# Four norms of a two-block transformer kernel: the eighth tile's squares summed on TensorE, the function table loaded ahead, and the second norm in three operations a tile

## The chip, the cores and the metric

The kernel is one program on one core of a Trainium2 chip. The time is the device time of that core in microseconds, the median of several executions. The engines are PE (TensorE), DVE (VectorE), ACT (ScalarE), POOL (GpSimd) and SP (SyncE), which run their own instruction streams and meet only at semaphores.

## The reference

Two transformer blocks run one after the other on a batch of one, with 512 tokens of 1024 channels in fp32. What matters here are four root-mean-square norms over the 1024 channels, each of which stands between two matrix products:

```python
x = x + gate1 * (merged @ w_o)                         # first block
y = rms_norm(x, norm2_w) * (1 + scale2) + shift2       # second norm
x = x + gate2 * ((gelu(conv(y @ up_a)) * (y @ up_v)) @ ffn_w_down)
xn = rms_norm_2(h, norm1_g)                            # third norm, second block
proj = xn @ w_in
...
h = h + merged @ w_out
hn = rms_norm_2(h, norm2_g)                            # fourth norm
ff = square(relu(hn @ w_ff1)); h = h + ff @ w_ff2
hg = rms_norm_2(h, norm3_g)                            # fifth norm
h = h + sigmoid(hg @ w_ple_gate + b) * (p @ w_ple)
```

with `rms_norm(x, w) = x * rsqrt(mean(x * x) + 1e-6) * w`.

## The kernel before

The activations lie transposed: a tile is 128 channels by 512 tokens, and eight tiles make the 1024 channels (`XR[0..7]` holds the residual stream). Every product is done in three passes: a weight block `wraw` is split into a rounded part `whi` (by ACT) and its remainder `wlo` (by DVE or POOL in turn), an activation tile into `hi` (ACT) and `lo` (DVE or POOL), and `mm3` runs hi\*hi, hi\*lo and lo\*hi on PE into one PSUM bank. `Split` objects name such pairs of tiles: `H2` is the input of the first block's feed-forward (`hhi`, `hlo`), `H3` that of the second block, `H4` and `H5` those of the fourth and fifth norm. The split of a weight block stands two blocks ahead of its use (`ahead`), so ACT, DVE and POOL issue it among their other work in program order. A product whose input has only just been made is `fresh`: its first two weight blocks are worked on together, channel tile by channel tile, so that each of the eight input tiles can be used as it comes.

The sum of squares of a norm is made while the product before it is evicted. For output tile m DVE adds the product to `XR[m]`, ACT squares it (`square`: tile 0 into `SQT`, the others in turn into `SCR[0]` and `SCR[1]`), and POOL adds it to `SQT` (`add_square`). When tile 7 has been added, `rsum` multiplies `SQT` by a 128x128 matrix of ones in fp32 on PE, which sums over the channels and puts the same sum into every partition. ACT then takes Ln and Exp of it (`inverse`), which gives the reciprocal root. Both need the table set `natural_log_exp_and_others`, which `act` loads just ahead of a Ln when another function's table is in the engine.

After the second and third norm the product can't begin before the normed tiles are made. Ahead of the fourth and fifth the gain alone is applied, and the reciprocal root multiplies the product's output, so PE goes on with the product as soon as it has issued the `rsum` matmul.

The second norm makes each of its eight tiles with five operations: DVE multiplies `XR[k]` by the reciprocal root into `A[:, 22 + k, :]` (`arena`), ACT applies scale and shift (`modcol(4, k)` and `modcol(3, k)`, in `mod`), ACT rounds it into `hhi`, and POOL (even k) or DVE (odd k) makes `hlo`. Between pairs of tiles each engine takes a step of `extra`, the product `p @ w_ple` (`ple`): PE multiplies two tiles (12 matmuls, of which the first step stands ahead of `rsum`), ACT splits the weight block two ahead, copies two banks into `SCR[3]` and `SCR[4]` and issues a DMA for each. The weight block split in the third of these steps is the first of the feed-forward (`fu0`), that in the fourth the second of `fu0`.

All matmuls have line 341 (`mm`), ACT's operations line 356 (`act`) and, for a table loaded by hand, line 352; `tensor_tensor` has line 359 and `scalar_tensor_tensor` line 367. In the changed kernel these helpers stand three lines further down.

Of the kernel before, what the change touches and what calls it, by code (L numbers as in the profile page):

```python
# [285 lines left out]
def build(nc, D, out, known):  # L286
# [5 lines left out]
    with ctx:  # L292
# [53 lines left out]
        log_exp = [False]  # L346

        def act(o, i, f, bias=0.0, scale=1.0, accum=None):
            kw = {} if accum is None else {"accum_out": accum}
            if f in (ACT.Ln, ACT.Exp):  # L350
                if not log_exp[0]:
                    ac.e.preload_act_table_set("natural_log_exp_and_others")  # L352
                log_exp[0] = True
            elif f not in (ACT.Copy, ACT.Identity, ACT.Square, ACT.Relu):
                log_exp[0] = False
            return ac.e.activation(o, i, f, bias=bias, scale=scale, **kw)  # L356
# [114 lines left out]
        HM = Split("hm", HP, odd_po)  # L471
        H2 = Split("h2", HP, even_po)
        PP = Split("pp", pair("pp", [(14, 2)], [(16, 1), (37, 1)]), lambda k: "ve")
# [506 lines left out]
        class Tensor(Stages):  # L980
# [460 lines left out]

            def rsum(self, sem, label, tile, dve_point):
                bk = PA.take(sem, label)
                pe.wait_ge(*PA.free(sem, label))
                pe.wait_ge(*at(*dve_point))
                mm(bk[:, :], ones, tile, True, True).then_inc(*inc(sem, label))
                PA.put((sem, label), "nr_act", "ln", label)

            def norm2(self, extra):
                self.rsum("nr_mm", "2", SQT, ("sq_po", "wo", 7))  # L1450
                for k in range(8):
                    if k % 2:
                        next(extra, None)

            def norm3(self):
                self.rsum("nr_mm", "3", SQT, ("sq_po", "fd", 7))

# [137 lines left out]
            def ff2_start(self):  # L1595
                self.rsum("nr_mm", "4", SQT, ("sq_po", "w2", 7))

            def norm5(self):
                self.rsum("nr_mm", "5", SQT, ("sq_po", "do", 7))

# [24 lines left out]
        class Scalar(Stages):  # L1625
# [354 lines left out]

            def ev_wo(self, m, bk):
                ac.wait_ge(*at("res_ve", "r1", m))
                self.square("wo", m, XR[m], SCR, lambda m: "po")

            def norm2(self, extra):
                self.inverse("2", SCR[2], ("nr_mm", "2"), PA.of("nr_mm", "2"), 1024)
                for k in range(8):
                    ac.wait_ge(*at("n2_ve", k))
                    ac.wait_ge(*at("mod_ve", 3, 0))
                    ac.wait_ge(*at("mod_ve", 4, 1))  # L1990
                    act(A[:, 22 + k, :], A[:, 22 + k, :], ACT.Identity, bias=modcol(3, k), scale=modcol(4, k)).then_inc(
                        *inc("n2_act", k))
                    ac.wait_ge(*at("n2_act", k))
                    self.high(H2, k, A[:, 22 + k, :])
                    if k % 2:
                        next(extra, None)
# [15 lines left out]

            def ev_fd(self, m, bk):
                ac.wait_ge(*at("res_ve", "r2", m))
                self.square("fd", m, XR[m], SCR, lambda m: "po")
# [231 lines left out]

            def ev_w2(self, m, bk):
                ac.wait_ge(*at("res_ve", "r3", m))
# [21 lines left out]
            def ev_do(self, p):  # L2271
                def f(m, bk):
                    if p == 3:
                        ac.wait_ge(*at("res_ve", "r4", 3, m))
# [42 lines left out]
        class Vector(Stages):  # L2317
# [415 lines left out]
            def norm2(self, extra):  # L2733
                ve.wait_ge(*at("nr_act", "ri", "2"))
                ve.wait_ge(*at("mix_po", 7))
                for k in range(8):
                    tt(ve, A[:, 22 + k, :], XR[k], SCR[2], ALU.mult).then_inc(*inc("n2_ve", k))
                    self.low(H2, k, A[:, 22 + k, :])
                    if k % 2:
                        next(extra, None)  # L2740
# [273 lines left out]
        class Gpsimd(Stages):  # L3014
# [14 lines left out]
            def add_square(self, stage, m, tmp):  # L3029
                if m:  # L3030
                    po.wait_ge(*at("sq_act", stage, m))
                    if m > 1:
                        po.wait_ge(*at("sq_po", stage, m - 1))
                    tt(po, SQT, SQT, tmp[m % 2], ALU.add).then_inc(*inc("sq_po", stage, m))
# [113 lines left out]

            def norm2(self, extra):
                for k in range(8):  # L3150
                    self.low(H2, k, A[:, 22 + k, :])
                    if k % 2:
                        next(extra, None)

# [221 lines left out]
```

## Time and profile before

| | |
|---|---|
| median of 3 runs | 2534.4 us (2533.56 to 2535.33) |
| profiled execution, its own time | 2541.82 us |
| its span, first to last instruction | 2539.9 us |
| busy: PE, DVE, ACT, POOL | 2360.4, 1082.5, 945.2, 698.6 us |
| mean granted clock of PE | 0.962 of 2.4 GHz |
| DMA | 220.64 MB, mean 87 GB/s |

Durations are read from the profiled execution, whose own time is 7.4 us above the median of the runs without a profile. The busy time of PE is 93% of the span. Matmul durations overlap: in a steady stream at the full clock a 512-column matmul is shown with 0.39 us and starts 0.23 us after the one ahead of it.

### The profile page before, as it was taken

Reading aid. Unit: us, or ns where it says so; the run is one execution under the profiler, and the core shown is the slowest. Engines: PE = TensorE matmul, PEld = TensorE weight load, DVE = VectorE, ACT = ScalarE, POOL = GpSimd, SP = SyncE. Lnnn points to the kernel's source line nnn. Section 1 sums busy time; section 2 is a strip of 40 time slices with the busy share of each in tenths; the row PEclk is TensorE's granted clock in tenths of the full one; section 3 lists DMA queues with packets and bytes.
Section 4 is the critical chain, followed back from the end, with each engine's and each line's share of the span. In section 5 each row is a group of like instructions: output and inputs, shape, how many; then the busy total and the mean of one; then the engine's idle time right before and its main releaser. Section 6 shows DMA issues by size and latency. Waiting matters only on the chain.

```text
span 2539.9 us, 27033 instructions
## 1 busy us (share of the span) xinstructions
PE 2360.4 (93%) x10928; PEld 1884.5 (74%) x10928; DVE 1082.5 (43%) x1588; ACT 945.2 (37%) x1364; POOL 698.6 (28%) x415
## 2 busy tenths in 40 slices
PE   8789999999889999899999887999999999999996
PEld 3577887986567677688888676787777777888875
DVE  2566664455443433433321599504443242322333
ACT  2554443223443433533322332334552333332334
POOL 1232243101211235222223241321232353332332
PEclk9899999999999899899999898999999999999998
DMA  8232222122122133333333422332221332333341
GB/s 264 66 92 59 75 75 75 51 70 59 38 67 69 44 105 90 120 96 96 92 99 100 124 75 58 92 100 67 84 67 58 109 91 79 106 91 97 100 124 50
DMA packets 347982, 220.64 MB, mean 87 GB/s; under 512 B 18393, under 2 KB 327244, under 8 KB 347860
## 3 DMA queue, kind: packets, MB, share of 16 engines
q1 hardware_dynamic: 338462, 202.31, 27.4%
q10 hardware_dynamic: 9398, 16.62, 2.0%
q8 instruction: 87, 1.43, 0.2%
q14 instruction: 35, 0.29, 0.0%
HBM read 210.49 MB, written 8.41 MB: 86 GB/s over the span
## 4 chain that ended last, share of the span: by engine, by line
PE 77%; DVE 11%; ACT 6%; POOL 3%; issue 3%; DMA 1%; ACTq 0%; SPq 0%; DVEq 0%; POOLq 0%
PE ps L341 75%; DVE arena L367 4%; DVE arena L359 2%; ACT arena L356 2%; POOL wlo L359 1%; DVE scr L367 1%; ACT scr L356 1%; PE ps L344 1%; ACT whi L356 1%; POOL arena L359 1%; ACT L352 1%; DVE wlo L359 1%; DVE scr L359 0%; DVE arena L364 0%; ACT L356 0%
## 5 line engine op out<-in xcount | busy, mean ns | idle before, releaser
L341 PE MATMUL ps<-hhi,whi 128*128 128x512 f32 x1664 | 679.2, 408 | 60.9 <-POOL wlo L359 39.3
L359 POOL TENSOR_TENSOR wlo<-wraw,whi 128x1024 fp32r<-128x1024 f32 (+1 forms) x163 | 390.6, 2396 | 1182.9 <-ACT whi L356 1182.9
L341 PE MATMUL ps<-hhi,wlo 128*128 128x512 f32 x1664 | 661.9, 398 | 0.0
L341 PE MATMUL ps<-hlo,whi 128*128 128x512 f32 x1664 | 661.8, 398 | 0.0
L356 ACT ACTIVATE whi<-wraw 128x1024 fp32r<-128x1024 f32 (+1 forms) x328 | 340.8, 1040 | 363.0 <-PE ps L341 296.7
L341 PEld LDWEIGHTS ps<-hhi,whi 128*128 128x128 f32 x1664 | 321.4, 193 | 146.3 <-issue 64.3
L341 PE MATMUL ps<-arena 128*128 128x128 f32 (+6 forms) x2304 | 342.9, 303 | 36.5 <-ACT arena L356 20.4
L359 DVE TENSOR_TENSOR wlo<-wraw,whi 128x1024 fp32r<-128x1024 f32 (+2 forms) x165 | 214.1, 1298 | 379.2 <-ACT whi L356 379.0
L341 PEld LDWEIGHTS ps<-hlo,whi 128*128 128x128 f32 x1664 | 322.0, 194 | 68.5 <-issue 3.7
L341 PEld LDWEIGHTS ps<-hhi,wlo 128*128 128x128 f32 x1664 | 320.6, 193 | 69.9
L341 PEld LDWEIGHTS ps<-arena 128*128 128x128 f32 (+1 forms) x2304 | 289.6, 199 | 69.3 <-issue 29.3
L356 ACT ACTIVATE arena<-ps 128x512 f32<-128x512 f32 (+5 forms) x223 | 116.0, 540 | 325.4 <-PE ps L341 285.5
L341 PE MATMUL ps<-h,whi 128*128 128x512 f32 x512 | 160.0, 394 | 1.1 <-POOL wlo L359 1.1
L367 DVE SCALAR_TENSOR_TENSOR arena<-arena,colv 128x512 f32<-128x512 f32 (+1 forms) x136 | 132.2, 977 | 16.3 <-ACT arena L356 12.6
L367 DVE SCALAR_TENSOR_TENSOR scr<-ps,colv,scr 128x511 f32<-128x511 f32 (+2 forms) x116 | 86.7, 749 | 121.3 <-ACT scr L356 118.7
L356 ACT ACTIVATE scr<-ps,colv 128x512 f32<-128x512 f32 x78 | 55.5, 712 | 217.0 <-PE ps L341 212.0
L359 DVE TENSOR_TENSOR arena<-ps,arena 128x512 f32<-128x512 f32 (+1 forms) x88 | 56.3, 640 | 150.6 <-PE ps L341 148.2
L359 DVE TENSOR_TENSOR scr<-ps,scr 128x512 f32<-128x512 f32 x86 | 59.1, 689 | 138.7 <-PE ps L341 137.1
L359 POOL TENSOR_TENSOR arena<-arena,scr 128x512 f32<-128x512 f32 x57 | 77.7, 1367 | 138.4 <-ACT scr L356 96.8
L341 PEld LDWEIGHTS ps<-h,whi 128*128 128x128 f32 x512 | 97.2, 190 | 22.6 <-issue 2.6
L341 PE MATMUL ps<-ff,whi 128*128 128x512 f32 x352 | 108.4, 389 | 0.0
L341 PE MATMUL ps<-h,wlo 128*128 128x512 f32 x256 | 100.4, 392 | 0.0
(190 smaller groups left out, 2654.4 us busy)
## 6 DMA issues: line engine op xcount, KB each, us to landing
wraw<-in_w_in_dram SPq DMA_DIRECT2D x99, 512.0 KB, 3.8
wraw<-in_w_ff_dram SPq DMA_DIRECT2D x64, 512.0 KB, 4.0
wraw<-in_ffn_w_up_dram SPq DMA_DIRECT2D x44, 512.0 KB, 3.9
wraw<-in_w_ada_dram SPq DMA_DIRECT2D x32, 512.0 KB, 3.9
wraw<-in_w_gate_dram SPq DMA_DIRECT2D x32, 512.0 KB, 3.9
arena<-in_w_ada_dram SPq DMA_DIRECT2D x8, 1024.0 KB, 10.9
wraw<-in_ffn_w_down_dram SPq DMA_DIRECT2D x16, 512.0 KB, 4.0
wraw<-in_w_branch_dram SPq DMA_DIRECT2D x16, 512.0 KB, 3.4
```

Source lines behind the costliest of these rows:

```text
L341: return pe.e.matmul(o, l, r, start=start, stop=stop)
L344: return pe.e.transpose(o, i, CST[0:n, C_ID:C_ID + n])
L352: ac.e.preload_act_table_set("natural_log_exp_and_others")
L356: return ac.e.activation(o, i, f, bias=bias, scale=scale, **kw)
L359: return q.e.tensor_tensor(o, a, b, op)
L367: return ve.e.scalar_tensor_tensor(out=o, in0=a, scalar=s, in1=b, op0=op0, op1=op1)
```

## The change

The change has four parts. `add_square` leaves tile 7 out, except in the last stage ("pg", the output norm, which is as before). In its place `rsum` issues two matmuls into the same bank: ones by `SQT`, which waits only for the addition of tile 6, and ones by `SCR[1]`, where ACT has put tile 7's squares. The table of Ln and Exp is loaded at output tile 0 of the product ahead of a norm (`ev_wo`, `ev_fd`, `ev_w2`, `ev_do`). The second norm has one `scalar_tensor_tensor` on DVE for `XR * scale * root`, one ACT operation that adds the shift and rounds into `hhi`, and one `scalar_tensor_tensor` on DVE that adds the shift again and subtracts `hhi`; DVE makes all eight `hlo` tiles, one tile behind, and POOL makes none.

```diff
+        def load_log_exp():
+            if not log_exp[0]:
+                ac.e.preload_act_table_set("natural_log_exp_and_others")
+            log_exp[0] = True
...
-        H2 = Split("h2", HP, even_po)
+        H2 = Split("h2", HP, lambda k: "ve")
...
-            def rsum(self, sem, label, tile, dve_point):
+            def rsum(self, label, stage):
...
-                pe.wait_ge(*at(*dve_point))
-                mm(bk[:, :], ones, tile, True, True).then_inc(*inc(sem, label))
+                pe.wait_ge(*at("sq_po", stage, 6))
+                mm(bk[:, :], ones, SQT, True, False)
+                pe.wait_ge(*at("sq_act", stage, 7))
+                mm(bk[:, :], ones, SCR[1], False, True).then_inc(*inc("nr_mm", label))
...
             def ev_wo(self, m, bk):
+                if m == 0:
+                    load_log_exp()
...
# ACT, norm2
-                    act(A[:, 22 + k, :], A[:, 22 + k, :], ACT.Identity, bias=modcol(3, k), scale=modcol(4, k)).then_inc(
-                        *inc("n2_act", k))
-                    ac.wait_ge(*at("n2_act", k))
-                    self.high(H2, k, A[:, 22 + k, :])
+                    act(H2.hi[k], A[:, 22 + k, :], ACT.Identity, bias=modcol(3, k)).then_inc(*inc("x_hi", "h2", k))
...
# DVE, norm2
-                for k in range(8):
-                    tt(ve, A[:, 22 + k, :], XR[k], SCR[2], ALU.mult).then_inc(*inc("n2_ve", k))
-                    self.low(H2, k, A[:, 22 + k, :])
+                for k in range(9):
+                    if k < 8:
+                        stt(A[:, 22 + k, :], XR[k], modcol(4, k), SCR[2], ALU.mult, ALU.mult).then_inc(*inc("n2_ve", k))
+                    if k:
+                        ve.wait_ge(*at(*H2.high_point(k - 1)))
+                        stt(H2.lo[k - 1], A[:, 21 + k, :], modcol(3, k - 1), H2.hi[k - 1].bitcast(F32), ALU.add,
+                            ALU.subtract).then_inc(*inc("x_lo_ve", "h2", k - 1))
...
             def add_square(self, stage, m, tmp):
-                if m:
+                if m and (m < 7 or stage == "pg"):
```

ACT's instructions where the second norm begins, before the change. `s_nr_mm` is the semaphore of the `rsum` matmul, `s_n2_ve` that of DVE's tiles; the `whi` operation is the weight split of the second `ple` step.

```order
L352 ACT_TABLE_LOAD [waits s_nr_mm]
L356 ACTIVATE scr<-ps,cst 128x512
L356 ACTIVATE scr<-scr 128x512 [waits s_nr_act]
L356 ACTIVATE arena<-arena,mod 128x512 [waits s_n2_ve]
L356 ACTIVATE hhi<-arena 128x512 [waits s_n2_act]
L356 ACTIVATE arena<-arena,mod 128x512 [waits s_n2_ve]
L356 ACTIVATE hhi<-arena 128x512 [waits s_n2_act]
L356 ACTIVATE whi<-wraw 128x512 [waits s_raw0]
L356 ACTIVATE scr<-ps 128x512 [waits s_pls_out0,s_mm]
L1979 DMA pls_dram<-scr 128x512 [waits s_ple_act]
```

The same place after the change: the table load is gone from it, and each tile has one operation in place of two.

```order
L359 ACTIVATE scr<-ps,cst 128x512 [waits s_nr_mm]
L359 ACTIVATE scr<-scr 128x512 [waits s_nr_act]
L359 ACTIVATE hhi<-arena,mod 128x512 [waits s_n2_ve] x2
L359 ACTIVATE whi<-wraw 128x512 [waits s_raw0]
L359 ACTIVATE scr<-ps 128x512 [waits s_pls_out0,s_mm]
L1985 DMA pls_dram<-scr 128x512 [waits s_ple_act]
L359 ACTIVATE scr<-ps 128x512 [waits s_pls_out1,s_mm]
L1985 DMA pls_dram<-scr 128x512 [waits s_ple_act]
L359 ACTIVATE hhi<-arena,mod 128x512 [waits s_n2_ve] x2
```

DVE's instructions of the second norm before the change, from the first tile to the second weight split.

```order
L359 TENSOR_TENSOR arena<-arena,scr 128x512 [waits s_mix_po,s_nr_act]
L359 TENSOR_TENSOR arena<-arena,scr 128x512
L359 TENSOR_TENSOR hlo<-arena,hhi 128x512 [waits s_x_hi]
L359 TENSOR_TENSOR arena<-arena,scr 128x512 x2
L359 TENSOR_TENSOR hlo<-arena,hhi 128x512 [waits s_x_hi]
L359 TENSOR_TENSOR wlo<-wraw,whi 128x1024 [waits s_w_hi]
L359 TENSOR_TENSOR arena<-arena,scr 128x512 x2
L359 TENSOR_TENSOR hlo<-arena,hhi 128x512 [waits s_x_hi]
L359 TENSOR_TENSOR arena<-arena,scr 128x512 x2
L359 TENSOR_TENSOR hlo<-arena,hhi 128x512 [waits s_x_hi]
L359 TENSOR_TENSOR wlo<-wraw,whi 128x1024 [waits s_w_hi]
```

And after it. All sixteen operations are now `scalar_tensor_tensor`, and the odd and the even `hlo` are both here; the remaining rows of the stage go on in the same way.

```order
L370 SCALAR_TENSOR_TENSOR arena<-arena,mod,scr 128x512 [waits s_mix_po,s_nr_act]
L370 SCALAR_TENSOR_TENSOR arena<-arena,mod,scr 128x512
L370 SCALAR_TENSOR_TENSOR hlo<-arena,mod,hhi 128x512 [waits s_x_hi]
L370 SCALAR_TENSOR_TENSOR arena<-arena,mod,scr 128x512
L370 SCALAR_TENSOR_TENSOR hlo<-arena,mod,hhi 128x512 [waits s_x_hi]
L370 SCALAR_TENSOR_TENSOR arena<-arena,mod,scr 128x512
L370 SCALAR_TENSOR_TENSOR hlo<-arena,mod,hhi 128x512 [waits s_x_hi]
L362 TENSOR_TENSOR wlo<-wraw,whi 128x1024 [waits s_w_hi]
L370 SCALAR_TENSOR_TENSOR arena<-arena,mod,scr 128x512
L370 SCALAR_TENSOR_TENSOR hlo<-arena,mod,hhi 128x512 [waits s_x_hi]
L370 SCALAR_TENSOR_TENSOR arena<-arena,mod,scr 128x512
```

DVE's work there has grown from four `hlo` tiles to eight, and its own two or three instructions a tile are next to each other; POOL, which had the other four and tile 7's squares, has only its weight splits left.

## Rows read from the trace of the kernel before

**Rows 1.** The page, part 4: shares of the chain that ended last.

```profile
PE 77%; DVE 11%; ACT 6%; POOL 3%; issue 3%; DMA 1%; ACTq 0%; SPq 0%; DVEq 0%; POOLq 0%
```

**Rows 2.** That chain around the second norm: start us, us, what.

```profile
1026.61 1.28 ACT L352
...
1043.80 1.05 ACT whi L356
...
1044.92 2.51 POOL wlo L359
...
1047.57 361.33 PE ps L341 x1581
```

**Rows 3.** The same chain around the third norm.

```profile
1410.41 1.27 POOL arena L359
...
1411.81 2.06 PE ps L341 x2
...
1413.88 1.28 ACT L352
...
1415.18 0.70 ACT scr L356
```

**Rows 4.** The same chain ahead of the fourth norm.

```profile
2107.57 1.32 POOL arena L359
```

**Rows 5.** Timeline of PE, in brackets its idle time before and what ended it.

```profile
1025.48 1.10 PE L341 MATMUL ps<-arena,cst 128*128 128x512 f32 x2 [0.25 <-POOL arena L359]
...
1435.20 0.47 PE L341 MATMUL ps<-hhi,whi 128*128 128x512 f32 x1 [1.81 <-DVE wlo L359]
...
1611.35 3.86 PE L341 MATMUL ps<-arena,cst 128*128 128x512 f32 x8 [1.39 <-ACT arena L356]
...
2109.03 2.04 PE L341 MATMUL ps<-arena,cst 128*128 128x512 f32 x2 [3.54 <-POOL arena L359]
...
2466.04 1.65 PE L341 MATMUL ps<-arena,cst 128*128 128x512 f32 x2 [3.53 <-POOL arena L359]
```

**Rows 6.** Timeline of ACT in the second norm.

```profile
1035.32 0.82 ACT L356 ACTIVATE arena<-arena,mod 128x512 f32<-128x512 f32 x1 [0.41 <-DVE arena L359]
...
1038.07 1.04 ACT L356 ACTIVATE whi<-wraw 128x1024 fp32r<-128x1024 f32 x1
```

**Rows 7.** Timeline of ACT at the last ff2 stage.

```profile
2425.19 0.72 ACT L356 ACTIVATE hhi<-arena,colv 128x512 fp32r<-128x512 f32 x1 [5.05 <-DVE arena L359]
2425.82 0.62 ACT L356 ACTIVATE arena<-arena 128x512 f32<-128x512 f32 x1
```

**Rows 8.** Timelines of DVE and POOL, at three places.

```profile
1045.13 2.83 DVE L359 TENSOR_TENSOR arena<-arena,scr 128x512 f32<-128x512 f32 x1
...
1505.25 6.81 DVE L367 SCALAR_TENSOR_TENSOR arena<-arena,colv 128x512 f32<-128x512 f32 x4
...
1511.48 2.78 POOL L359 TENSOR_TENSOR wlo<-wraw,whi 128x1024 fp32r<-128x1024 f32 x1
...
2425.95 0.75 DVE L367 SCALAR_TENSOR_TENSOR hlo<-arena,colv,hhi 128x512 fp32r<-128x512 f32 x1 [0.79 <-ACT hhi L356]
```

**Rows 9.** Stretches: from:to, length, busy us by engine, granted PE clock, DMA share, GB/s.

```profile
1435.80:1438.90 3.10, 3.10 (x9) 2.39 (x8) 1.70 (x3) 1.78 (x3) 1.49 (x1) 0.50 1.04 330
1611.30:1616.00 4.70, 4.65 (x13) 2.24 (x14) 0.00 (x0) 2.45 (x4) 0.00 (x0) 1.00 0.01 5
2109.00:2114.70 5.70, 5.67 (x11) 3.80 (x12) 0.00 (x0) 3.55 (x4) 0.00 (x0) 0.50 0.01 3
2466.00:2470.00 4.00, 3.96 (x9) 2.65 (x10) 0.00 (x0) 2.24 (x3) 0.00 (x0) 0.57 1.01 375
```

**Rows 10.** Timeline of ACT where the table would now be loaded.

```profile
990.40 1.05 ACT L356 ACTIVATE whi<-wraw 128x1024 fp32r<-128x1024 f32 x1
...
1304.98 0.63 ACT L356 ACTIVATE arena<-arena 128x512 f32<-128x512 f32 x1 [3.75 <-DVE arena L367]
...
2075.22 0.72 ACT L356 ACTIVATE h<-arena,colv 128x512 fp32r<-128x512 f32 x1 [1.89 <-DVE arena L359]
```

More of the change, by code:

```diff
@@ L350, in act @@
             if f in (ACT.Ln, ACT.Exp):
-                if not log_exp[0]:
-                    ac.e.preload_act_table_set("natural_log_exp_and_others")
-                log_exp[0] = True
+                load_log_exp()
             elif f not in (ACT.Copy, ACT.Identity, ACT.Square, ACT.Relu):
@@ L1440, in ple @@
                 yield from self.linear("ple", self.nothing)
-            def rsum(self, sem, label, tile, dve_point):
-                bk = PA.take(sem, label)
-                pe.wait_ge(*PA.free(sem, label))
-                pe.wait_ge(*at(*dve_point))
-                mm(bk[:, :], ones, tile, True, True).then_inc(*inc(sem, label))
-                PA.put((sem, label), "nr_act", "ln", label)
+            def rsum(self, label, stage):
+                bk = PA.take("nr_mm", label)
+                pe.wait_ge(*PA.free("nr_mm", label))
+                pe.wait_ge(*at("sq_po", stage, 6))
+                mm(bk[:, :], ones, SQT, True, False)
+                pe.wait_ge(*at("sq_act", stage, 7))
+                mm(bk[:, :], ones, SCR[1], False, True).then_inc(*inc("nr_mm", label))
+                PA.put(("nr_mm", label), "nr_act", "ln", label)
             def norm2(self, extra):
-                self.rsum("nr_mm", "2", SQT, ("sq_po", "wo", 7))
+                self.rsum("2", "wo")
                 for k in range(8):
@@ L1455, in norm3 @@
             def norm3(self):
-                self.rsum("nr_mm", "3", SQT, ("sq_po", "fd", 7))
+                self.rsum("3", "fd")
             def conv(self):
@@ L1595, in ff2_start @@
             def ff2_start(self):
-                self.rsum("nr_mm", "4", SQT, ("sq_po", "w2", 7))
+                self.rsum("4", "w2")
             def norm5(self):
-                self.rsum("nr_mm", "5", SQT, ("sq_po", "do", 7))
+                self.rsum("5", "do")
             def turn(self, m):
@@ L1981, in ev_wo @@
             def ev_wo(self, m, bk):
+                if m == 0:
+                    load_log_exp()
                 ac.wait_ge(*at("res_ve", "r1", m))
@@ L1989, in norm2 @@
                     ac.wait_ge(*at("mod_ve", 3, 0))
-                    ac.wait_ge(*at("mod_ve", 4, 1))
-                    act(A[:, 22 + k, :], A[:, 22 + k, :], ACT.Identity, bias=modcol(3, k), scale=modcol(4, k)).then_inc(
-                        *inc("n2_act", k))
-                    ac.wait_ge(*at("n2_act", k))
-                    self.high(H2, k, A[:, 22 + k, :])
+                    act(H2.hi[k], A[:, 22 + k, :], ACT.Identity, bias=modcol(3, k)).then_inc(*inc("x_hi", "h2", k))
                     if k % 2:
@@ L2013, in ev_fd @@
             def ev_fd(self, m, bk):
+                if m == 0:
+                    load_log_exp()
                 ac.wait_ge(*at("res_ve", "r2", m))
@@ L2248, in ev_w2 @@
             def ev_w2(self, m, bk):
+                if m == 0:
+                    load_log_exp()
                 ac.wait_ge(*at("res_ve", "r3", m))
@@ L2273, in f @@
                     if p == 3:
+                        if m == 0:
+                            load_log_exp()
                         ac.wait_ge(*at("res_ve", "r4", 3, m))
@@ L2735, in norm2 @@
                 ve.wait_ge(*at("mix_po", 7))
-                for k in range(8):
-                    tt(ve, A[:, 22 + k, :], XR[k], SCR[2], ALU.mult).then_inc(*inc("n2_ve", k))
-                    self.low(H2, k, A[:, 22 + k, :])
+                ve.wait_ge(*at("mod_ve", 4, 1))
+                for k in range(9):
[5 more added lines that the diff above has]
+                            ALU.subtract).then_inc(*inc("x_lo_ve", "h2", k - 1))
                     if k % 2:
@@ L3147, in ev_wo @@
                 self.add_square("wo", m, SCR)
[L3149 to L3153, printed above, removed]
+            norm2 = Plan.norm2
             def ev_fv(self, m, bk):
```

## The prediction

> **What bounds the kernel now.** I read the chain that ended last first. PE holds 77% of it [rows 1], so a step of another engine counts only where PE stands still for it. The change touches four such places.
>
> At the second norm the chain goes from the `rsum` matmul (start 1025.48, [rows 5]) over the table load (1026.61) and, after ACT's work on six tiles, to the weight split `whi` at 1043.80, POOL's `wlo` at 1044.92 and PE at 1047.57, from where PE runs for 361 us without a stall [rows 2]. What ends last there is not a normed tile but the weights: the second block of `fu0` stands in ACT's queue behind six tiles and three `ple` steps. At the third norm every step is on the chain: POOL's addition (1410.41), `rsum` (1411.81), the load (1413.88), Ln (1415.18) [rows 3]. Ahead of the fourth and fifth norm PE idles 3.54 and 3.53 us until POOL's addition is through [rows 5], and then goes on with a product that is ready; Ln and Exp there run beside it.
>
> **The second norm, part by part.** *Sum and table.* POOL's addition is hardly in the way: PE comes out of the first `ple` step only 0.25 us before it starts `rsum` [rows 5]. After the change it issues two fp32 matmuls there. Four of them in a row take 3.86 us [rows 5], 0.97 each, so the pair that starts at about 1025.1 ends at 1027.0, 0.4 later than the single one. The load of 1.28 us that follows [rows 2] is gone: Ln starts at 1027.0 in place of 1027.9, a gain of 0.9.
>
> *ACT's queue.* Two tiles take ACT 1038.07 - 1035.32 = 2.75 us [rows 6], with four operations. After it they are two, each with one pointer operand; the nearest row is the 0.72 us operation after which the next starts 0.63 us later [rows 7], so 1.26 us a pair. Three pairs stand ahead of the `whi` at 1043.80: 3 x 1.49 = 4.5 us. What lies between the pairs (weight split, two copies, two DMAs) is the same.
>
> *DVE.* It now does sixteen operations of 0.75 us [rows 8] in place of twelve, one tile behind. Ahead of the sixth tile it has, after a weight split, three of them in a row where ACT wants the tile after two: 0.7 us late. The first tile's multiplication is slower by less than 0.1. All of DVE's seventeen operations, from about 1028.4 on, are through by 1044; PE wants tile 7 only after 42 of the 48 `fu0` matmuls, 9.7 us at 0.23 each after it resumes, so `hlo` itself is not late.
>
> *DVE and POOL together.* A DVE multiplication beside POOL's split of 1044.92 took 2.83 us, and four `scalar_tensor_tensor` beside POOL's operations took 6.81, which is 1.70 each in place of 0.75; a POOL split beside DVE's work took 2.78 in place of 2.51 [rows 2, 8]. Two of POOL's splits fall among the sixteen operations. The first can hold the fourth tile up by 0.3, the second is itself the last link and loses 0.3: 0.6 in all. The Trainium skill ("SBUF — State Buffer", section "SBUF: two separate sides") has a rule for it that speaks against this change: of a DVE operation with two SBUF inputs and a GpSimd operation, the first to start holds the shared ports for its whole length, and the other stands. By that rule DVE stands for the rest of each of POOL's splits, which gives the same delays as above, since only these two splits are left to POOL.
>
> Sum for the second norm: 0.9 + 4.5 - 0.7 - 0.1 - 0.6 = **4.0 us**; PE resumes at 1043.6. The bounds: 0 if DVE is held up throughout (below), 5.4 if neither the sixth tile nor POOL costs anything.
>
> **The third norm.** The first `rsum` matmul runs while DVE and ACT deal with tile 7. The second starts when the square is done, about 1410.5 in place of 1411.81: 1.3 us. It took 2.06 us here [rows 3], at half clock after an idle stretch; at 1025.48 it took 1.10 [rows 5]. With PE idle for hardly a microsecond ahead of it I expect the latter: 0.95. The load goes: 1.3. Sum **3.6 us** (2.6 if the clock is still low). DVE, ACT, POOL and PE go through H3's tiles as before, only earlier, and the convolutions behind it start from the product. The Trainium skill ("ScalarE: Activation LUTs", section "What ACT_TABLE_LOAD costs") gives a switch 2.66 us, with a drain of 1.38 behind the load. By it the two loads on the path would give 2.8 us more. The trace does not bear it out: the load at 1413.88 lasts 1.28 and Ln starts at 1415.18, 0.02 after it [rows 3].
>
> **The fourth and fifth norm.** PE no longer waits for POOL's 1.32 us with 0.07 ahead of it [rows 4]: **1.4 us** each. The added matmul runs in the idle time. There is a second part. After these idle stretches PE ran at 0.50 of its clock, the level of 1.2 GHz, for 5.7 us at 2109.00, and at a mean of 0.57 for 4.0 us at 2466.00 [rows 9]. The 11 records of the first are one `rsum` and nine matmuls, 0.97 + 9 x 0.23 = 3.0 us at the full clock, so 2.7 are lost; the 9 of the second are 0.97 + 7 x 0.23 = 2.6, so about 1.5 are lost. After the change the 3.5 us of idle time are cut in two by a matmul of 0.97 and shortened by 1.4, which leaves some 1.2 to 1.4 in one piece. After an idle time of 1.39 (at 1611.35) the clock stayed at 1.00; after one of 1.81 (at 1435.20) it fell to 0.50 for the 3.1 us from 1435.80 [rows 5, 9]. The new gap is nearest to the first: I take the 2.7 + 1.5 = **4.2 us** as gained, with 0 as the other bound.
>
> **What costs nothing.** The loads themselves are moved, not saved. In `ev_w2` ACT waits 1.89 us and in `ev_fd` 3.75 us for DVE where the 1.28 would go [rows 10]. In `ev_wo` the load stands ahead of the weight split at 990.40 [rows 10], and that block's turn on PE comes after two others of 24 matmuls, 11 us; without that cover it would be 1.3. In `ev_do` the table is in the engine already: no load stands between Ln and Exp of the fourth norm and those of the fifth. No DMA is added; SP's loads wait for weight splits and come earlier with them.
>
> **Sum.** 4.0 + 3.6 + 1.4 + 1.4 + 4.2 = 14.6 us. The profiled execution took 2541.8 us, so it would be 2527.2; that execution is 7.4 above the median of the plain runs, so I expect **2519.8 us** there. About 0.2%, 5.1 us, is what a measurement of this kernel can tell from no change.
>
> **The rivals.**
> 1. *The clock falls all the same* ahead of the fourth or fifth norm, or is still low for `rsum` in the third. For it speaks that 1.81 us were enough once. It costs up to 4.2 + 0.95: 2521 to 2525.
> 2. *DVE becomes the bound of the second norm.* If its operations all took the 1.70 us of [rows 8], the eleven ahead of the sixth tile would end at 1028.4 + 18.7 = 1047.1, and with 0.6 for the tile, 1.05 for `whi` and 2.8 for POOL, PE would resume at 1051.6, 4.0 after 1047.57. The gain would be 14.6 - 8.0 = 6.6: 2527.8. Against it: POOL has two splits left in that stretch, so DVE is alone for most of it.
> 3. *Slower than before.* The same mechanism, but so strong that the last `hlo` tile holds PE. Before, tile 7 was wanted at about 1059. To eat up the other 10.6 us it must come at 1069.8, which is (1069.8 - 1028.4) / 17 = 2.4 us for each DVE operation. Were all like the one of 2.83 [rows 8], it would come at 1076.5: 17 us lost, 10.6 gained, 2541 us. Only one row is that slow.
> 4. *The change does not do what it says:* a Square or Copy between tile 0 and Ln asks for another table, and the load comes back to where it was. That costs 1.3 in the second and third norm: 2522.4. Before, the operations between Exp and the end of the second norm ran with no load among them (the first of the four listings in the section on the change), so these functions are served by the table that is in.
> 5. *More than forecast.* PE also starts `fu0` and the third norm's product at the low clock, and the idle stretches there become shorter. If one or both of the low stretches shrink, 2 to 4 us come on top: 2516 to 2518.
>
> **How the numbers follow.** The forecast with all terms within a microsecond 0.46; rival 1 0.32; rival 5 0.11; rival 2 0.04; rival 4 0.03; rival 3 0.01; something unseen that takes most of the gain 0.03. From 2516.5 to 2525.0 lie the forecast, rivals 1 and 4 and most of rival 5, about 0.87. Faster by over 0.2% are all but rival 3 and the unseen: 0.95; within 0.2% 0.035; slower 0.015.
>
> **What the changed profile would show.** Ln of the second and third norm right behind `rsum`, no load on the chain. Two ACT operations of about 0.7 us per pair of tiles, and PE resuming some 18 us after the second `rsum` matmul started in place of 22. In the third norm about 1.1 us for the second `rsum` matmul. Ahead of the fourth and fifth norm two idle pieces that sum to about 1.2 to 1.4 us, with the granted clock at 1.00 behind them. The prediction is wrong if DVE's operations are long beside POOL's splits, if PE resumes after 1046 at the second norm, or if the clock behind the fourth and fifth norm is low.

## The result, and the profile after it

| | before | after |
|---|---|---|
| median of plain runs beside each other | 2534.54 us (2533.56 to 2535.33) | 2516.89 us (2515.87 to 2520.84) |
| ratio of the medians, 95% interval | | 0.9931 (0.9919 to 0.9943) |
| profiled execution, its own time | 2541.82 us | 2517.34 us |
| its span | 2539.9 us | 2515.5 us |
| mean granted clock of PE | 0.962 | 0.970 |

The change gains 17.65 us; 14.6 were forecast (2519.8 us). The time lies inside the range, 2516.5 to 2525.0, 0.4 us from its fast end.

One thing has to be read first. The two spans differ by 24.4 us, not by 17.6, and 6.85 of that lie ahead of everything that was edited: DVE's last eviction ahead of the second norm ends at 1023.30 before and at 1016.45 after, and the code up to there is the same apart from one table load. It is about the difference in what the profiled executions stand above their medians: 7.3 us before, 0.45 after. So the stages below are counted from that point. At later points the kernel after is ahead by:

| point in the program | lead, us | gained since the last point | forecast |
|---|---|---|---|
| PE resumes `fu0` (1036.14) | 4.58 | second norm 4.58 | 4.0 |
| last eviction ahead of norm 3 (1397.17) | 5.65 | stretch behind norm 2 1.07 | 0 |
| Ln of norm 3 (1399.05) | 9.28 | third norm 3.63 | 3.6 |
| last eviction ahead of norm 4 (2089.11) | 10.26 | between 0.98 | 0 |
| product behind norm 4, 11.4 us after the sum's second matmul (2101.89) | 14.48 | fourth norm 4.22 | 1.4 + 2.7 |
| product behind norm 5, 11.4 us after it (2454.71) | 17.56 | fifth norm 3.11 (less 0.03) | 1.4 + 1.5 |
| end (2515.50) | 17.55 | 0 | 0 |

The sum, 17.55, is close to the 17.65 of the medians. The page of the kernel after, part 1 (busy us and share by engine) and part 4 (the chain's shares, against [rows 1]):

```profile
PE 2346.0 (93%) x10936; PEld 1873.5 (74%) x10936; DVE 1086.0 (43%) x1592; ACT 940.3 (37%) x1356; POOL 688.6 (27%) x407
...
PE 76%; DVE 11%; ACT 6%; issue 3%; POOL 3%; DMA 1%; ACTq 0%; SPq 0%; DVEq 0%; POOLq 0%
```

The chain around the second norm (start us, us, what), where [rows 2] had the load, `whi` at 1043.80 and POOL's `wlo` at 1044.92:

```profile
1020.14 0.70 ACT scr L359
...
1022.32 0.69 ACT hhi L359
...
1031.82 0.02 issue
1031.85 0.02 ACT hhi L359
...
1032.47 1.05 ACT whi L359
...
1033.59 2.42 POOL wlo L362
...
1036.14 3.89 PE ps L341 x9
```

The chain ends with the same last link as before, the weight split: `whi` by ACT, `wlo` by POOL, then PE. The load is not on it. The piece ahead of the last `whi` is an `hhi` that waited for DVE. The timeline of ACT shows the three pairs of tiles:

```profile
1020.14 0.69 ACT L359 ACTIVATE scr<-ps,cst 128x512 f32<-128x512 f32 x1 [1.00 <-PE ps L341]
...
1022.32 1.39 ACT L359 ACTIVATE hhi<-arena,mod 128x512 fp32r<-128x512 f32 x2 [0.82 <-DVE arena L370]
...
1026.17 1.45 ACT L359 ACTIVATE hhi<-arena,mod 128x512 fp32r<-128x512 f32 x2 [0.40 <-ACT scr L359]
...
1029.78 0.60 ACT L359 ACTIVATE scr<-ps 128x512 f32<-128x512 f32 x1 [0.73 <-DMA pls_dram<-scr]
...
1030.78 0.72 ACT L359 ACTIVATE hhi<-arena,mod 128x512 fp32r<-128x512 f32 x1 [0.41 <-DVE arena L370]
1031.85 0.72 ACT L359 ACTIVATE hhi<-arena,mod 128x512 fp32r<-128x512 f32 x1 [0.34 <-DVE arena L370]
1032.47 1.04 ACT L359 ACTIVATE whi<-wraw 128x1024 fp32r<-128x1024 f32 x1
```

The pairs take 1.29, 1.35 and, the third, 1.69 us from first `hhi` to `whi`, where [rows 6] had 2.75. The last is longer because DVE brings the sixth tile 0.34 us late. `scr<-ps` at 1029.78 waits 0.73 us for a DMA out of the same buffer; a step earlier that copy waits 0.46. The timeline of PE (against [rows 5]; in brackets the idle time before and what ended it):

```profile
1018.22 1.02 PE L341 MATMUL ps<-arena,cst 128*128 128x512 f32 x2
1019.08 1.02 PE L341 MATMUL ps<-scr,cst 128*128 128x512 f32 x2
...
1036.14 0.77 PE L341 MATMUL ps<-hhi,whi 128*128 128x512 f32 x1 [5.18 <-POOL wlo L362]
...
1396.22 1.02 PE L341 MATMUL ps<-arena,cst 128*128 128x512 f32 x2
1397.88 1.13 PE L341 MATMUL ps<-scr,cst 128*128 128x512 f32 x2 [0.65 <-ACT scr L359]
...
2088.22 1.02 PE L341 MATMUL ps<-arena,cst 128*128 128x512 f32 x2
2090.44 1.13 PE L341 MATMUL ps<-scr,cst 128*128 128x512 f32 x2 [1.20 <-ACT scr L359]
...
2441.03 1.02 PE L341 MATMUL ps<-arena,cst 128*128 128x512 f32 x2
2443.26 1.12 PE L341 MATMUL ps<-scr,cst 128*128 128x512 f32 x2 [1.20 <-ACT scr L359]
```

The first matmul of each pair runs in what was idle time. The second waits for ACT's square alone: 0.65 us in the third norm, 1.20 in the fourth and fifth, where one piece of 3.54 and 3.53 stood. The second fp32 matmul of norm 3 takes 1.13 us in place of 2.06. Ln there starts at 1399.05, right behind it. The stretches (columns as in [rows 9]: after the busy times the granted clock, the DMA share, GB/s):

```profile
1036.20:1039.30 3.10, 3.10 (x8) 2.42 (x9) 2.86 (x4) 2.02 (x3) 0.00 (x0) 0.50 0.84 253
2085.00:2097.00 12.00, 10.80 (x44) 7.93 (x43) 3.17 (x4) 4.40 (x6) 3.74 (x2) 1.00 0.30 84
2438.00:2450.00 12.00, 10.80 (x45) 7.93 (x44) 2.98 (x4) 4.22 (x6) 3.57 (x2) 1.00 0.73 242
```

Around norms 4 and 5 the granted clock is 1.00, the level of 2.4 GHz, where [rows 9] had 0.50 and 0.57. Behind norm 2 it is still at the low level, but for 3.1 us.

### The profile page after: what moved, and what is told of

It reads as the page before. It is cut to its first block, busy times and chain, and to the rows that moved or that the text cites. A ratio compares the mean times of both kernels' runs of the same rounds, so it can differ in the third digit from the quotient of the medians.

```text
span 2515.5 us, 27034 instructions
## 1 busy us (share of the span) xinstructions
PE 2346.0 (93%) x10936; PEld 1873.5 (74%) x10936; DVE 1086.0 (43%) x1592; ACT 940.3 (37%) x1356; POOL 688.6 (27%) x407
## 4 chain that ended last, share of the span: by engine, by line
PE 76%; DVE 11%; ACT 6%; issue 3%; POOL 3%; DMA 1%; ACTq 0%; SPq 0%; DVEq 0%; POOLq 0%
PE ps L341 75%; DVE arena L370 4%; DVE arena L362 2%; ACT arena L359 2%; POOL wlo L362 1%; DVE scr L370 1%; PE ps L344 1%; ACT scr L359 1%; ACT whi L359 1%; DVE wlo L362 1%; ACT L350 1%; POOL arena L362 1%; DVE arena L367 1%; DVE scr L362 0%; ACT L359 0%
## 5 line engine op out<-in xcount | busy, mean ns | idle before, releaser
L362 POOL TENSOR_TENSOR arena<-arena,scr 128x512 f32<-128x512 f32 x53 | 71.7, 1357 | 126.1 <-ACT scr L359 84.5
```

Of the source, the lines that this page charges most:

```text
L362: return q.e.tensor_tensor(o, a, b, op)
```

## The experiments

The parts of the change were run alone first, as edits of the kernel before (medians against 2534.13 us on the same chip).

**The sum alone.** Only `rsum` and `add_square` as in the change.

```diff
+                mm(bk[:, :], ones, SQT, True, False)
+                pe.wait_ge(*at("sq_act", stage, 7))
+                mm(bk[:, :], ones, SCR[1], False, True).then_inc(*inc("nr_mm", label))
...
-                if m:
+                if m and (m < 7 or stage == "pg"):
```

> The first part of the change alone: tile 7's squares go straight into the sum; table and second norm as before. My account (terms add, and the clock stays up behind the fourth and fifth norm): second norm 0.4 us slower (two matmuls in place of one behind the first ple step), third 2.3 faster (1.3 of waiting, 0.95 for a matmul at the full clock), fourth 1.4 + 2.7, fifth 1.4 + 1.5, so 8.9 us faster than before. Rival, the clock falls all the same because it was the whole change that shortened the idle time: 4 to 5 us faster.

Measured: 2524.54 us, ratio 0.9962 (0.9950 to 0.9975), 9.6 faster. From the landmarks: norm 2 loses 0.38 (the added matmul, forecast 0.4), norm 3 gains 2.35, norm 4 4.20, norm 5 3.10. The whole gain of the fourth and fifth norm is this part. The profiled execution is ahead by 11.8 in all, because another 2.3 come between norms 3 and 4, where nothing is edited (below).

**The table alone.** Only the early loads.

```diff
+                if m == 0:
+                    load_log_exp()
```

> The second part alone: the table of Ln and Exp is loaded at tile 0; sums and second norm as before. My account: the load of 1.28 us goes from the path of the second and third norm, and nothing at the fourth and fifth, where Ln and Exp run beside the product: 2.6 us faster than before. Rival, a switch costs 2.66 us as the Trainium skill has it (ScalarE: Activation LUTs, What ACT_TABLE_LOAD costs): 5.3 us faster. Rival, the load only moves a wait: 0.

Measured: 2530.65 us, 0.9986 (0.9977 to 0.9996), 3.5 faster. At norm 2 the gain is 1.28, the length of the load. At norm 3 it is another 2.23, more than a load, and PE's row says why:

```profile
1400.96 1.10 PE L341 MATMUL ps<-arena,cst 128*128 128x512 f32 x2 [2.94 <-POOL arena L362]
```

With the same 2.94 us of idle time as in the kernel before, this fp32 matmul took 1.10 where it took 2.06 there [rows 3]. So 0.95 of it is the clock, which happened to stay up. Two more differences stand where nothing is edited: 1.0 gained right behind norm 2 and 1.05 lost between norms 3 and 4; 3.6 are left at the end. The Trainium skill ("ScalarE: Activation LUTs", section "What ACT_TABLE_LOAD costs") gives a switch 2.66 us with its drain, which would be 5.3 for the two loads; the stage readings, 1.28 each, do not bear the drain out. The rival of 5.3 us did not come true, and that of 0 neither.

**The second norm alone.**

```diff
-                    act(A[:, 22 + k, :], A[:, 22 + k, :], ACT.Identity, bias=modcol(3, k), scale=modcol(4, k)).then_inc(
-                        *inc("n2_act", k))
+                    act(H2.hi[k], A[:, 22 + k, :], ACT.Identity, bias=modcol(3, k)).then_inc(*inc("x_hi", "h2", k))
```

> The third part alone: the second norm in three operations a tile, with DVE making all eight hlo tiles; sums and table as before. My account from the two profiles: 3.7 us less until PE resumes with the feed-forward's second weight block. Whether the 1.1 us that the low clock behind it cost less in the changed kernel's profile belongs to this part is open: 3.7 without, 4.8 with it. Rival, DVE's sixteen operations and POOL's weight splits hinder each other more without the rest of the change: 0 to 2 us faster.

Measured: 2531.32 us, 0.9988 (0.9979 to 0.9997), 2.8 faster, below the 3.7 that was expected. PE resumes 3.70 us earlier, as expected, and at the end of the profiled execution 3.5 are left. The low clock behind the norm costs as much as before, so the other 1.1 us in question are not this part's.

**Sum and table together.**

```diff
+                mm(bk[:, :], ones, SQT, True, False)
...
+                if m == 0:
+                    load_log_exp()
```

> The first and the second part together, the second norm in five operations as before. If the parts simply add: 8.9 + 2.6 = 11.5 us faster than before, and the whole change beats it by what the third part gives alone (3.7 to 4.8). If the sum and the table hid each other (POOL's addition could have covered a load), it would differ from the sum of the two by about 1.3 us.

Measured: 2519.51 us, 0.9940 (0.9927 to 0.9952), 14.6 faster. Norm 2 gains 0.89; with the 3.70 of the part before that is 4.59, and the whole change shows 4.58: at this place the parts add. The profile has norm 3 at 3.63, norm 4 at 4.20, norm 5 at 3.09. Where it is above the 11.5 of a plain sum, the profile has 1.2 us that come right behind norm 2 and 2.2 between norms 3 and 4. The medians of the whole program add less well than the stages: 9.6, 3.5 and 2.8 make 15.9, and the whole change gains 17.65.

The next four (before 2534.57 us on their chip) test the clock and the queue.

**Both matmuls late.** The changed kernel, with the first matmul behind the last square as well.

```diff
                 pe.wait_ge(*PA.free("nr_mm", label))
+                pe.wait_ge(*at("sq_act", stage, 7))
                 pe.wait_ge(*at("sq_po", stage, 6))
```

> The changed kernel, except that the first of the two fp32 matmuls of each norm's sum also waits for tile 7's square, so that both stand behind it instead of one in the idle time and one behind it. Changed kernel 2516.9 us. Plain theory (a step on the path costs its length): the first matmul, 0.97 to 1.02 us, comes onto the path at the third, fourth and fifth norm and not, or by 0.1, at the second, where PE comes late anyway: 2.9 us slower than the changed kernel, 2519.8. Rival: the pieces of idle time matter for the clock, not only their sum. Ahead of the fourth and fifth norm the idle time is now one piece of 2.2 us in place of two of about 0.2 and 1.2; if that piece lets the clock fall, the stretch behind each is at the low clock as in the kernel before (2.7 and 1.5 us), 4.2 more: 2524.0. Second rival: the fp32 pair costs nothing because the next product's matmuls are held by something else: 2516.9.

Measured: 2520.79 us (2519.82 to 2521.82), 3.9 slower than the changed kernel. The plain theory had 2.9, the rival 7.1. Norm 3 loses 0.87 of its gain, norms 4 and 5 lose 2.5 each: one matmul, 0.97, and 1.5 of clock. Some 1.9 come back between norms 3 and 4, where the two kernels are the same (below). The timeline of PE and the stretch behind:

```profile
2088.95 1.10 PE L341 MATMUL ps<-arena,cst 128*128 128x512 f32 x2 [2.10 <-issue]
2089.88 1.45 PE L341 MATMUL ps<-scr,cst 128*128 128x512 f32 x2
```

```profile
2089.00:2095.00 6.00, 6.00 (x16) 3.96 (x17) 0.11 (x1) 2.26 (x3) 1.26 (x1) 0.72 0.05 14
```

The clock of 0.72 over these six microseconds lies between the 0.50 of the kernel before and the 1.00 of the changed one. It came down while the second fp32 matmul ran (1.45 us in place of about 1.0). So the rival was right in kind and too high in size: where the first matmul stands matters for the clock too, not only for the path.

**Fillers in the kernel before.** Three matmuls of ones by constants in the idle time ahead of norms 4 and 5, POOL's addition waited for as before; the sum's own matmul overwrites them.

```diff
                 pe.wait_ge(*PA.free(sem, label))
+                if label in "45":
+                    for _ in range(3):
+                        mm(bk[:, :], ones, CST[:, 0:S], True, True)
                 pe.wait_ge(*at(*dve_point))
```

> The kernel before, with three more fp32 matmuls of ones by constants (0.97 us each at full clock) into the bank of the sum, ahead of the fourth and of the fifth norm; the sum's own matmul overwrites what they leave. POOL's addition is waited for as before. Clock theory: of the 17.6 us of the change about 4.2 are the clock, which falls because PE idles 3.5 us there; with PE kept busy in that time it stays at 1.00 and 2.7 + 1.5 = 4.2 us come back, 2529.9 against 2534.1. If the three matmuls take longer than the 3.5 us in which they hide, at most 0.5 less. Rival: it was the shorter wait alone that gained, and the granted clock there goes by something else (the load over a longer time): no difference, 2534.1, or the time of the fillers as a loss.

Measured: 2529.26 us (2528.30 to 2530.26), 0.9977 (0.9968 to 0.9986), 5.3 faster.

```profile
2098.06 2.74 PE L341 MATMUL ps<-cst 128*128 128x512 f32 x6
2101.67 1.13 PE L341 MATMUL ps<-arena,cst 128*128 128x512 f32 x2 [0.87 <-POOL arena L359]
```

```profile
2095.00:2106.00 11.00, 10.13 (x38) 6.75 (x37) 3.02 (x4) 5.11 (x7) 2.51 (x2) 1.00 0.31 89
2450.00:2461.00 11.00, 10.13 (x38) 6.72 (x37) 2.89 (x3) 3.51 (x5) 3.30 (x3) 1.00 0.72 232
```

The landmarks give 2.85 for norm 4 and 1.70 for norm 5, with the granted clock at 1.00 in both stretches: the 2.7 and 1.5 of the prediction, with not one wait shortened. PE did work that nobody needs, and the kernel became faster.

**Fillers in the changed kernel.** Five ahead of the second block of `fu0`, four behind norm 3's sum.

```diff
+                                if k == 0 and n and l.X is H2:
+                                    self.fill("f2", 5)
...
+                if label == "3":
+                    self.fill("f3", 4)
...
+            def fill(self, key, n):
+                bk = PA.take(key)
+                b = PA.banks[PA.made[key,]]
+                pe.wait_ge(*PA.free(key))
+                for _ in range(n):
+                    mm(bk[:, :], ones, CST[:, 0:S], True, True)
+                b.held = False
```

> The changed kernel, with PE kept busy in idle time where it still comes out at the low clock: five fp32 matmuls of ones by constants into a free bank ahead of the first matmul of the second block of the first feed-forward product (the end of the second norm), and four behind the third norm's sum. Changed kernel 2516.9 us. Clock theory: the low stretches behind the second and third norm (8 to 9 matmuls at 0.43 us in place of 0.23 behind each) shrink or go, 1.7 to 2 us each, minus what the fillers stick out of the idle time: 2 to 4 us faster, 2513 to 2515. Rival: the fillers are at the low clock themselves (2.06 us each) and hold up the product's first tiles, or the clock behind goes by phase: no difference or up to 4 us slower, 2517 to 2521.

Measured: 2515.55 us (2514.99 to 2516.96), 1.3 faster than the changed kernel's 2516.89, where 2 to 4 were expected. The profiled executions of the two have the same lead at the end, 17.5, so the 1.3 is not explained by its stages. Behind norm 2 the low stretch is gone, and the lead grows by 1.63. Behind norm 3 it is gone too, and bought nothing. The same piece of program, from the first matmul of the product to its third weight block, in the changed kernel and in this one:

```profile
1403.33:1419.07 15.74, 13.46 (x49) 10.60 (x49) 9.27 (x11) 6.24 (x9) 4.50 (x8) 0.85 0.43 134
```

```profile
1401.07:1416.78 15.71, 11.90 (x49) 8.70 (x49) 9.25 (x11) 6.24 (x9) 4.48 (x8) 1.00 0.43 135
1416.90:1421.20 4.30, 4.30 (x13) 3.35 (x14) 2.74 (x4) 2.26 (x3) 1.98 (x1) 0.60 1.07 317
```

15.74 us at a mean clock of 0.85, and 15.71 at 1.00. PE waits there for the normed tiles at full clock too, so a slow PE costs nothing. And the low level came right behind instead, 0.60 over 4.3 us at 1416.90, where PE is the bound: that took 1.6 us back, all that the fillers behind norm 2 had gained.

**The steps ahead of their pairs.** On all four engines the `ple` step stands ahead of each pair of tiles.

```diff
                 for k in range(8):
-                    if k % 2:
+                    if k % 2 == 0:
                         next(extra, None)
```

> The changed kernel, with each step of the product that is worked on between the second norm's pairs of tiles put ahead of its pair instead of behind it, on PE, ACT, DVE and POOL: the split of the second block's weights of the first feed-forward product stands one pair of tiles earlier in ACT's queue. Changed kernel 2516.9 us. Theory that ACT's queue ahead of that weight split sets the end of the second norm: the split comes one pair of tiles earlier, 1.3 to 1.7 us, 2515.2 to 2515.6. Rival: something else takes its place at once (the steps' banks or DMAs, since the first step then stands directly behind Ln and Exp with its PE work not done, or the last normed tiles): 0, 2516.9, or slower by a step that ACT waits for, up to 2 us.

Measured: 2515.66 us (2514.53 to 2516.24), 1.2 faster. PE resumes 1.59 us earlier. So ACT's queue ahead of the weight split was the bound, and moving it by a pair gave a pair's worth. Of that 0.1 is left at the end of the profiled execution (a lead of 17.7 against 17.5): behind norm 2 the low stretch is longer, 11 slow matmuls in place of 8, and less is gained between norms 3 and 4. The gain at the edited place is shown; that of the median is not traced to it. The chain shows what bounds it now:

```profile
1022.08 4.21 DMA pls_dram<-scr
...
1026.37 0.61 ACT scr L359
...
1028.64 1.05 ACT whi L359
...
1029.76 2.65 POOL wlo L362
```

The longest pieces on it are no longer tiles: two DMAs out of the copies' buffers, this one of 4.21 us, which the next copy into the same buffer waits for.

The last four ran on one chip (before 2534.96 us), the unedited changed kernel among them.

**The changed kernel again.**

> The changed kernel once more, unedited, beside the other three on one chip: 2516.9 us by both theories; it shows how far differences of 1 to 2 us can be trusted.

Measured: 2516.54 us (2514.58 to 2517.24). The two medians of this kernel are 0.35 us apart, and single runs of it range from 2514.58 to 2520.84.

**Fillers where PE is the bound.** The kernel with the steps ahead of their pairs, and five fillers ahead of the second block of `fu0` and two ahead of the third block of norm 3's product (`cg1`).

```diff
+                                if k == 0 and n and l.X is H2:
+                                    self.fill("f2", 5)
...
+                        if name == "cg1":
+                            self.fill("f3", 2)
```

> The changed kernel with the steps ahead of their pairs (2515.7 us in the earlier run, against 2516.9 for the changed kernel), and five fp32 matmuls of ones by constants in PE's 5.4 us of idle time ahead of the second block of the first feed-forward product, and two ahead of the third block of the third norm's product, where PE idles 2 to 3 us and the clock in some kernels falls for 3.4 us. The low stretch behind the third norm's sum is left alone, because the filled and the unfilled kernel took the same 15.7 us from the first of those matmuls to the third block. Theory: 12 matmuls at 0.43 us in place of 0.23 behind the second norm (2.4 us less) and 1.6 us behind the third norm: 2.4 to 4 us less than 2515.7, 2511.7 to 2513.3. Rival: clock time that is filled at one place comes back at the next idle stretch (as at the third norm before, where the fall only moved): 0 to 1.6, 2514 to 2516.

Measured: 2512.10 us (2511.91 to 2513.31), 0.9909 (0.9895 to 0.9923), 4.4 faster than the changed kernel beside it.

```profile
1028.42 4.45 PE L341 MATMUL ps<-cst 128*128 128x512 f32 x10
1033.87 0.47 PE L341 MATMUL ps<-hhi,whi 128*128 128x512 f32 x1 [1.00 <-POOL wlo L362]
```

```profile
1028.42:1038.00 9.58, 8.58 (x29) 5.15 (x28) 9.32 (x12) 6.47 (x10) 2.52 (x1) 1.00 0.62 192
1415.20:1420.00 4.80, 4.80 (x21) 3.99 (x22) 3.10 (x5) 2.39 (x3) 2.11 (x1) 1.00 1.06 311
```

Both places are at 1.00. PE resumes where it did without the fillers, and the lead at the next point is 2.3 us larger. Between norms 3 and 4 another 2.1 us are gained against the kernel without them, and the lead at the end is 22.0 against 17.7 there.

**The split made by DVE.** The steps ahead of their pairs, and the remainder split of `fu0`'s second block by DVE, that of the next block by POOL.

```diff
+            odd = i % 2
+            if i - W.index["fu0", P, 0] in (0, 1):
+                odd = not odd
+            return "w_lo_ve" if odd else "w_lo_po"
```

> The changed kernel with the steps ahead of their pairs (2515.7 us), and with the remainder split of the second weight block of the first feed-forward product made by DVE and that of the next block by POOL, in place of the other way round. Theory: that split is the last link ahead of PE at the second norm; POOL took 2.64 us for it and held one DVE operation for 2.83, DVE took 1.23 for an equal one elsewhere: 1.2 to 1.5 us less, 2514.2 to 2514.5. Rival: DVE is busy with its sixteen operations and comes to the split late, or the normed tiles come late behind it: 0 or slower by up to 1.2, 2515.7 to 2516.9.

Measured: 2513.29 us (2511.37 to 2515.23), 0.9911 (0.9897 to 0.9926).

```profile
1030.01 1.22 DVE L362 TENSOR_TENSOR wlo<-wraw,whi 128x1024 fp32r<-128x1024 f32 x1 [1.07 <-ACT whi L359]
...
1031.38 0.77 PE L341 MATMUL ps<-hhi,whi 128*128 128x512 f32 x1 [3.95 <-DVE wlo L362]
```

PE resumes 1.09 us earlier than with POOL's split. The median is 2.4 us lower, where 1.2 to 1.5 were expected, but the profiled execution (the slowest of the five) gives the 1.1 us back: 0.5 right behind norm 2, with 14 slow matmuls in place of 11, and 0.6 between norms 3 and 4. How much of the 2.4 is the split's stays open.

**All of it.**

```diff
+            if i - W.index["fu0", P, 0] in (0, 1):
...
+                                    self.fill("f2", 5)
...
+                            self.fill("f3", 2)
```

> All of it: steps ahead of their pairs, the swapped split, and both groups of fillers. If the parts add: 2515.7 less 1.3 (split) less 2.4 to 4 (fillers) = 2510.4 to 2512.0. With DVE's split PE's idle time there is only some 4 us, so five fillers of 0.9 us (4.45 for the five in the earlier run) may hold PE up by up to 0.5. Rival: the clock and the split each give less than alone, 2513 to 2515.

Measured: 2511.87 us (2510.52 to 2514.39), 0.9908 (0.9893 to 0.9923), 4.7 faster than the changed kernel beside it and no different from the 2512.10 without the swapped split. PE resumes 1.03 us earlier than there, and 1.9 us less is gained between norms 3 and 4. So the swapped split is worth about 1 us where PE resumes, and no whole-program time here shows it clear of the clock.

## Why the prediction was right, and where it was short

**The mechanism** was right at all four norms, but for one half of a term in the second: which engine stands at the shared ports. What was short is the sum, by 3.0 us: 0.6 in the second norm, 2.05 in two stretches that were put at nothing, 0.3 at norms 4 and 5.

**Second norm: 4.58 in place of 4.0.** *Sum and table*: Ln starts 0.91 us earlier against the eviction (3.69 us behind it in place of 4.60); 0.9 was the forecast. *ACT's queue, DVE and the first of POOL's splits*, from Ln to the last `whi`: 15.90 us before [rows 2], 12.33 after, 3.57 gained; forecast were 4.5 - 0.7 - 0.1, less 0.3 of contention, 3.4. Its pieces are off in both directions: the pairs' lateness is 0.4, not 0.7, and a DMA that the second copy waits for takes 0.3 that was not seen. *The last link* is the term that was mis-sized most: 0.3 lost was forecast, 0.1 was gained. The rows of DVE and POOL at the two splits, against [rows 8]:

```profile
1024.41 1.78 DVE L370 SCALAR_TENSOR_TENSOR hlo<-arena,mod,hhi 128x512 fp32r<-128x512 f32 x1
...
1033.71 2.83 DVE L370 SCALAR_TENSOR_TENSOR arena<-arena,mod,scr 128x512 f32<-128x512 f32 x1
...
1024.30 1.34 POOL L362 TENSOR_TENSOR wlo<-wraw,whi 128x512 fp32r<-128x512 f32 x1 [10.02 <-ACT whi L359]
1033.59 2.40 POOL L362 TENSOR_TENSOR wlo<-wraw,whi 128x1024 fp32r<-128x1024 f32 x1 [7.95 <-ACT whi L359]
```

POOL starts first and is not slowed (2.40 us). DVE starts 0.12 us later and ends 0.55 after POOL, 2.83 in all; at the first split it also ends 0.55 after POOL, 1.78 in all. With the steps ahead of their pairs the order is the other one: a DVE operation, started at 1029.46, is under way when POOL's split starts at 1029.76, and the split takes 2.65. This is what the rule of the Trainium skill says ("SBUF — State Buffer", section "SBUF: two separate sides"): the first to start holds the shared ports for its whole length, the other stands. By that rule alone the 0.3 at POOL's end should not have stood in the sum: the one that stands is DVE, and DVE's next tile is not on the path there. The prediction wrote that the rule gives the same delays; it does not.

**Third norm: 3.63 in place of 3.6**, made of 1.3 (wait), 0.95 (clock) and 1.3 (load), as the parts run alone show: 2.35 for the sum, 1.28 for the load. But the 0.95 is less sure than the forecast put it: the table alone got it as well, with the old idle time of 2.94 us.

**Fourth and fifth norm: 4.22 and 3.11 in place of 4.1 and 2.9.** Both terms stand. That the clock is worth 2.7 and 1.5 is shown without the shorter wait by the fillers in the kernel before (2.85 and 1.70), and with it by the late first matmul, which loses 1.5 at each. (The prediction's 1.5 is 4.0 - 2.6 = 1.4 by its own rows, and the fillers gained 1.70 there.)

**The step that was short** is the one that left the clock elsewhere at nothing and put it into rival 5: "if one or both of the low stretches shrink, 2 to 4 us come on top". 2.05 came, and the shorter idle time that it named does not account for them. That the time is still inside the range is in part luck: the forecast counted none of these 2.05 us, and 0.4 more would have put it outside. *Behind norm 2* PE was at the low level from 1047.57 to 1053.25 before, 13 matmuls at 0.43 us, and to about 1039.3 after, 8 of them: 5 x 0.20 = 1.0. The idle time ahead became shorter (6.05 to 5.18 us), but that does not set it: with the same 5.18 the second norm alone has 14 slow matmuls, and with 5.60 the table alone has 8. *Between norms 3 and 4* the changed kernel escaped one low stretch, that of [rows 9] from 1435.80. From the product's first matmul to the end of PE's first long wait (6.6 us), before and after, with the same 360 matmuls (columns as in [rows 9]):

```profile
1419.46:1514.40 94.94, 86.54 (x360) 70.59 (x361) 79.75 (x88) 32.47 (x45) 27.61 (x18) 0.93 0.36 105
1403.33:1496.64 93.31, 84.42 (x360) 69.07 (x361) 79.49 (x88) 32.59 (x45) 27.88 (x18) 0.96 0.37 107
```

94.94 us before and 93.31 after. The experiments have nearly the same two numbers: 93.3 the sum alone, the second norm alone, both matmuls late, sum and table together, the fillers in the kernel before and the two kernels with fillers where PE is the bound; 94.9 the table alone, the fillers in the changed kernel, the steps ahead with and without the swapped split. Further on there is a second such place, ahead of the fourth norm: from the end of PE's wait at 1881.33 to that at 2043.12 are 161.8 us after, 161.3 before, and 160.5 to 160.6 with the sum alone, sum and table, both matmuls late, and the first of the two kernels with fillers where PE is the bound. So 0.5 of the 1.6 is lost again there, and the kernel with both matmuls late gets 1.3 of its 1.9 there. Whether the clock falls at such a place can't be told from the idle time ahead of it alone: at the first, 2.97 us left it up with both matmuls late, and 1.81 brought it down before [rows 5]. What decides it was not settled.

**The rivals.** 1 did not come true: in all ten profiles in which the idle time of norms 4 and 5 comes in pieces of 1.2 us and below, the clock stayed at 1.00 there; in the two experiments that left it at 3.5 it fell as before. 2 and 3 did not either: only two of DVE's sixteen operations were long. 4 did not: no load stands at the norms. 5 did in size.

## What to carry to other kernels

Where PE idles for some microseconds ahead of a step and then is the bound, look at the granted clock behind the idle time as well as at the wait: here the clock was 4.2 of the 7.3 us at two norms, and useless matmuls in the idle time alone brought it back. Put them only where PE is the bound afterwards; where it waits for tiles anyway they buy nothing, and the clock can fall at the next stall instead. And where two engines meet at the shared ports, ask which of them is on the path and who starts first: the one that starts second pays.

## What the runs showed of the hardware that was not expected

A 512-column fp32 matmul of a sum with the same 2.94 us of idle time ahead of it took 2.06 us in one kernel and 1.10 in another. Low stretches behind the second norm had 8 matmuls or 14 with the same 5.18 us of idle time, and the one ahead of the convolutions came or stayed away, worth 1.6 us, and another 1.3 us came or went at a second unedited place; two kernels that differ by less than 2 us can owe that to it. A DVE operation that starts 0.1 to 0.4 us behind a POOL split ends 0.55 us after it, with a short split (1.34) as with a long one (2.40 and 2.64).
